# DeltaNet decays from gate sums in DRAM, loaded as broadcast rows

## What is computed

```python
def chunk_gated_delta(q, k, v, g, beta, s0):
    gc = jnp.cumsum(g, axis=-1)
    decay = jnp.exp(jnp.where(incl, gc[..., :, None] - gc[..., None, :], -jnp.inf))
    kb = k * beta[..., None]
    a_mat = (jnp.where(strict, jnp.einsum('bhnid,bhnjd->bhnij', kb, k) * decay, 0.0)
             + jnp.eye(DN_CHUNK, dtype=jnp.float32))
    ...
    qk = jnp.einsum('bhnid,bhnjd->bhnij', q, k) * decay

    def step(s, inp):
        v_new = u_i - jnp.einsum('bhcd,bhde->bhce', w_i, s)
        o_i = (jnp.einsum('bhcd,bhde->bhce', q_i * jnp.exp(g_i)[..., None], s)
               + jnp.einsum('bhij,bhje->bhie', qk_i, v_new))
```

## Time and profile before

| | us |
|---|---|
| median of 3 runs | 2942.37 |
| the runs | 2937.52 to 2944.89 |
| the profiled execution: its time | 2940.39 |
| the profiled execution: span of its instructions | 2938.8 |
| TensorE busy in it | 2628.8 |
| VectorE busy | 1885.0 |
| ScalarE busy | 1367.0 |
| GpSimd busy | 569.2 |

### The profile page before, as it was taken

One profiled execution on the slowest core, in us unless ns is written; L12 is line 12 of the kernel. 1 busy time (PEld: TensorE's weight loads), 2 busy tenths in 40 slices (PEclk: granted clock), 3 DMA queues, 4 the chain that ended last, 5 costly groups with the idle time before them and its releaser, 6 DMA issues. The chain is left out here.

```text
span 2938.8 us, 51977 instructions
## 1 busy us (share of the span) xinstructions
PE 2628.8 (89%) x17133; PEld 2420.6 (82%) x17133; DVE 1885.0 (64%) x3056; ACT 1367.0 (47%) x2263; POOL 569.2 (19%) x716
## 2 busy tenths in 40 slices
PE   2458999999999699999999999898999999998697
PEld 2458999999989598888888888898888888887597
DVE  3878888888853547665766566434576657665433
ACT  1024334434333535655565556323656555655522
POOL 2302222222211101221122112102112211221110
PEclk9999999999999799999999999999999999999899
DMA  8565666666653142222222222333222222221042
GB/s 237 188 222 201 233 230 229 228 229 232 227 177 128 57 147 69 74 69 68 68 75 71 69 70 68 123 124 133 65 75 68 71 71 68 75 71 50 20 156 93
DMA packets 115499, 362.09 MB, mean 123 GB/s; under 512 B 29056, under 2 KB 31232, under 8 KB 114560
## 3 DMA queue, kind: packets, MB, share of 16 engines
q1 hardware_dynamic: 69408, 252.74, 25.3%
q0 software_dynamic: 21200, 87.04, 8.8%
q10 hardware_dynamic: 24848, 21.76, 2.7%
HBM read 345.76 MB, written 15.73 MB: 123 GB/s over the span
## 5 line engine op out<-in xcount | busy, mean ns | idle before, releaser
L450 PE MATMUL bank<-h_hi,w_hi 128*128 128x384 f32 x2576 | 981.6, 381 | 48.0 <-DVE h_lo L1114 33.6
L452 PE MATMUL bank<-h_hi,w_lo 128*128 128x384 f32 x2576 | 872.3, 339 | 0.0
L451 PE MATMUL bank<-h_lo,w_hi 128*128 128x384 f32 x2576 | 871.2, 338 | 0.0
L418 DVE TENSOR_TENSOR w_lo<-raw,w_hi 128x1024 fp32r<-128x1024 f32 x418 | 555.2, 1330 | 443.4 <-ACT w_hi L410 406.9
L410 ACT ACTIVATE w_hi<-raw 128x1024 fp32r<-128x1024 f32 x418 | 442.0, 1060 | 455.8 <-PE bank L452 423.4
L450 PEld LDWEIGHTS bank<-h_hi,w_hi 128*128 128x128 f32 x2576 | 491.8, 191 | 71.3 <-issue 45.8
L451 PEld LDWEIGHTS bank<-h_lo,w_hi 128*128 128x128 f32 x2576 | 493.5, 192 | 13.5 <-issue 7.2
L452 PEld LDWEIGHTS bank<-h_hi,w_lo 128*128 128x128 f32 x2576 | 489.2, 190 | 0.0
L1079 DVE SCALAR_TENSOR_TENSOR ada_terms<-raw_ada,cond_rows 128x1024 f32<-128x1024 f32 x256 | 312.5, 1221 | 10.1 <-DMA raw_ada<-in_late 5.6
L450 PE MATMUL bank<-y_hi,w_hi 128*128 128x384 f32 x768 | 262.8, 342 | 29.2 <-DVE y_lo L1184 22.0
L451 PE MATMUL bank<-y_lo,w_hi 128*128 128x384 f32 x768 | 262.0, 341 | 0.0
(11 more groups left out here) (218 smaller groups left out, 3862.3 us busy)
## 6 DMA issues: line engine op xcount, KB each, us to landing
raw<-in_stream SPq DMA_DIRECT2D x482, 512.0 KB, 3.3
raw_ada<-in_late POOLq DMA_DIRECT2D x128, 512.0 KB, 3.6
x_kept<-y POOLq DMA_DIRECT2D x2, 3072.0 KB, 9.8
y<-x_kept POOLq DMA_DIRECT2D x2, 3072.0 KB, 10.3
bias<-in_rpb ACTq DMA_DIRECT2D x16, 256.0 KB, 6.5
S<-in_state ACTq DMA_DIRECT2D x16, 256.0 KB, 2.6
out_state_out<-s_out ACTq DMA_DIRECT2D x16, 256.0 KB, 2.1
y<-in_x ACTq DMA_DIRECT2D x1, 3072.0 KB, 20.0
```

The costliest lines, as they stand in the source:

```text
L418: nc.vector.tensor_tensor(w_lo[:, mk % SPLIT_SLOTS, :], raw[:, raw_n % RAW_SLOTS, :], w_hi[:, mk % SPLIT_SLOTS, :].bitcast(F32), ALU.subtr ...
L450: nc.tensor.matmul(bank[:, 0:T], w_hi[:, slot, w], hi[:, kt, :], start=kt == 0, stop=False)
L451: nc.tensor.matmul(bank[:, 0:T], w_hi[:, slot, w], lo[:, kt, :], start=False, stop=False)
L452: last = nc.tensor.matmul(bank[:, 0:T], w_lo[:, slot, w], hi[:, kt, :], start=False, stop=kt == KT - 1)
```

## The change

The gate sums are no longer formed once per head by products with triangles of ones. The phase `ba` forms them once for all heads: the table `gc` (tokens on the partitions) is a copy of the first `sums` product, and six products of the gates with the masks `le` and `ge` (`rows0`, `rows1`) give the same sums with the tokens along the row. ScalarE copies these and writes them to DRAM (`gc_rows`, 16 heads of 1536 numbers) with four DMAs. At the start of each head ScalarE, behind the load of the state, issues a load of the head's 6 KB to all 128 partitions (768 KB), into `decays`, one buffer that now holds the three `decay[c]`. Then:

- `broad` stands first in the list: ScalarE waits for that load and takes exp of chunks 1 and 2 straight from SBUF to `q_dec[c]`.
- `decay`: GpSimd subtracts the column of sums `gc_now` and cuts at 0, in place (four instructions per chunk), and ScalarE takes exp in place.
- The products of `decay` and `broad`, the masks of GpSimd and `g_now` are gone; `gc_now` is copied by VectorE at the start of the head. The ring's list is four places shorter (five gone, one place unused).
- `unit` has weight 3 and stands behind all three decays; with the other weights this leaves `norms`, `gram` and all that follows at the same part as before.

The diff, cut to its core:

```diff
-_chain = [(5, ("norms",)), (2.5, ("decay", 0)), (2, ("decay", 1)), (1.5, ("broad", 1)), (0, ("unit",)), (2, ("decay", 2)),
-          (1.5, ("broad", 2)), (1, ("gram", 0)), (2, ("gram", 1)), (2, ("gram", 2)), (1, ("values", 0)),
+_chain = [(0, ("broad", 1)), (0, ("broad", 2)), (5, ("norms",)), (2.5, ("decay", 0)), (2, ("decay", 1)), (2, ("decay", 2)),
+          (3, ("unit",)), (1, ("gram", 0)), (2, ("gram", 1)), (2, ("gram", 2)), (1, ("values", 0)),
           (1, ("values", 1))]
 for _stage in range(len(INVERT) - 1):
     _chain += [(3 if _stage < 2 and c < 2 - _stage else 2 if _stage < 2 else 1, ("invert", _stage, c)) for c in range(CHUNKS)]
...
+PRODUCTS += [("unused", "act")] * (-len(PRODUCTS) % RING)
...
-        g_now = sb("g_now", [P, CHUNKS, 2, 2])
+        gc_now = sb("gc_now", [P, CHUNKS, 2, 2])
+        gc = sb("gc", [P, CHUNKS, 2, DN_V_HEADS])
...
-        decay = [region.take(f"decay{c}", [P, 4, P]) for c in range(CHUNKS)]
+        decays = region.take("decays", [P, CHUNKS, 4, P])
+        decay = [decays[:, c, :, :] for c in range(CHUNKS)]
-        g_mask = [inv["c", c] for c in range(CHUNKS)]
+        gcT = overlay.take("gcT", [P, T])
-                                 "pool_waits", "v_out", "cache_k_in", "cache_v_in", "x0_in", "state_in", "state_out", "y_out")}
+                                 "pool_waits", "gc_out", "gc_in", "v_out", "cache_k_in", "cache_v_in", "x0_in", "state_in", "state_out", "y_out")}
...
+        def gc_loaded(eng, phase, turn):
+            eng.wait_ge(s["gc_in"], 16 * (turn + {"dn0": 1, "dn1": GROUP + 1, "dnE": 2 * GROUP}[phase]))
...
+            while PRODUCTS[n][0] == "unused":
+                n -= RING
...
+                for d, mask in enumerate(("le", "ge")):
+                    for c in range(CHUNKS):
+                        mm = nc.tensor.matmul(banks[6 + d][:, c * P:(c + 1) * P], bg[:, c, :], K[mask],
+                                              start=True, stop=True)
+                    done("pe", f"rows{d}", mm)
+
             def dn(pe, phase, turn):
                 for item in DN_PLANS[phase]:
                     what, arg = item[0], item[1] if len(item) > 1 else None
                     if what == "part":
                         multiply(pe, phase, turn, arg, item[2], h_hi, h_lo)
-                    elif what == "decay":
-                        wait_steps(pe, turn, ("pool", f"g_mask{arg}", True), ring_free(f"decay{arg}"))
-                        for d, mask in enumerate(("gt", "lt")):
-                            mm = nc.tensor.matmul(ring(f"decay{arg}")[:, 2 * d * P:(2 * d + 2) * P], K[mask],
-                                                  g_mask[arg][:, 2 * d:2 * d + 2, :].rearrange("p v i -> p (v i)"),
-                                                  start=True, stop=True)
-                        done("pe", f"decay{arg}", mm)
-                    elif what == "broad":
-                        wait_steps(pe, turn, ring_free(f"broad{arg}"))
-                        mm = nc.tensor.matmul(ring(f"broad{arg}")[:], K["ones"],
-                                              g_mask[arg][:].rearrange("p v i -> p (v i)"), start=True, stop=True)
-                        done("pe", f"broad{arg}", mm)
                     elif what == "norms":
                         for n in range(2):
                             wait_steps(pe, turn, ("pool", f"square{n}", True), ring_free(f"ss{n}"))
...
                     wait_steps(act, turn, ("pe", f"sums{n}"))
+                    if n == 0:
+                        done("act", "gc", nc.scalar.activation(gc[:].rearrange("p c d h -> p (c d h)"),
+                                                               banks[3][:, 0:CHUNKS * 2 * DN_V_HEADS], ACT.Copy))
                     done("act", f"table{n}", nc.scalar.activation(dst[:].rearrange("p c d h -> p (c d h)"),
                                                                   banks[3 + n][:, 0:CHUNKS * 2 * DN_V_HEADS], ACT.Exp))
+                for d in range(2):
+                    rows = slice(64 + 32 * d, 96 + 32 * d)
+                    wait_steps(act, turn, ("pe", f"rows{d}"))
+                    done("act", f"rows{d}", nc.scalar.activation(gcT[rows, :], banks[6 + d][rows, 0:T], ACT.Copy))
+                for d in range(2):
+                    wait_steps(act, turn, ("act", f"rows{d}"))
+                    for v in range(2):
+                        dst = bass.AP(dram["gc"].tensor, (2 * d + v) * P, [[CHUNKS * 4 * P, DN_K_HEADS], [4 * P, CHUNKS], [1, P]])
+                        src = gcT[64 + 32 * d + v:96 + 32 * d:2, :].rearrange("h (c i) -> h c i", c=CHUNKS)
+                        act.dma_start(dst, src).then_inc(s["gc_out"], 16)
             def dn(act, phase, turn):
                 head, _, _, row = heads(phase, turn)
...
+                    act.wait_ge(s["gc_out"], 16 * 4)
+                    act.dma_start(decays[:].rearrange("p c u i -> p (c u i)"),
+                                  dram["gc"][bass.ds(head, 1), :].broadcast_to([P, CHUNKS * 4 * P]))\
+                        .then_inc(s["gc_in"], 16)
                 def copy(name, dst, src, *others):
                     wait_steps(act, turn, ("pe", name), *others)
...
-                        wait_steps(act, turn, ("pe", f"decay{arg}"), ("pe", "outB", 1))
-                        done("act", f"decay{arg}", nc.scalar.activation(decay[arg][:].rearrange("p u i -> p (u i)"),
-                                                                        ring(f"decay{arg}")[:], ACT.Exp))
+                        wait_steps(act, turn, ("pool", f"below{arg}"))
+                        done("act", f"decay{arg}", nc.scalar.activation(decay[arg], decay[arg], ACT.Exp))
-                        wait_steps(act, turn, ("pe", f"broad{arg}"))
-                        done("act", f"broad{arg}", nc.scalar.activation(q_dec[arg][:].rearrange("p u i -> p (u i)"),
-                                                                        ring(f"broad{arg}")[:], ACT.Exp))
+                        gc_loaded(act, phase, turn)
+                        wait_steps(act, turn, ("pe", "outB", 1))
+                        done("act", f"broad{arg}", nc.scalar.activation(q_dec[arg][:], decay[arg], ACT.Exp))
...
+                    wait_steps(dve, turn, ("pool", "below2", True))
+                    done("dve", "gc_now", nc.vector.tensor_copy(gc_now[:], gc[:, :, :, bass.ds(2 * head, 2)]))
-                    elif what == "squares" and next_head is not None:
-                        wait_steps(dve, turn, ("pool", "g_mask2", True))
-                        done("dve", "g_now", nc.vector.tensor_copy(
-                            g_now[:], bg[:, :, 64:P].rearrange("p c (d h) -> p c d h", d=2)[:, :, :,
-                                                                                           bass.ds(2 * next_head, 2)]))
...
-                        wait_steps(dve, turn, ("dve", f"gram{c}"), ("act", f"decay{c}"), ("pe", f"broad{max(c, 1)}"),
-                                   ("pe", "applyB", True))
+                        wait_steps(dve, turn, ("dve", f"gram{c}"), ("act", f"decay{c}"), ("pe", "applyB", True))
...
-                    mask_steps(pool, turn)
...
-            def mask_steps(pool, turn, *which):
-                for c in range(CHUNKS):
-                    wait_steps(pool, turn, ("dve", "g_now"), *which)
-                    lone()
-                    for u in range(4):
-                        d, v = u // 2, u % 2
-                        i = nc.gpsimd.tensor_scalar(g_mask[c][:, u, :], K["le" if d == 0 else "ge"],
-                                                    g_now[:, c, d, v:v + 1], 1.0, ALU.mult, ALU.mult)
-                    done("pool", f"g_mask{c}", i)
...
-                        mask_steps(pool, turn, ("pe", "applyB"))
+                    elif what == "decay":
+                        gc_loaded(pool, phase, turn)
+                        wait_steps(pool, turn, ("dve", "gc_now"), *([("act", f"broad{arg}")] if arg else []))
+                        lone()
+                        for u in range(4):
+                            i = nc.gpsimd.tensor_scalar(decay[arg][:, u, :], decay[arg][:, u, :],
+                                                        gc_now[:, arg, u // 2, u % 2:u % 2 + 1], 0.0, ALU.subtract, ALU.min)
+                        done("pool", f"below{arg}", i)
...
+        dram["gc"] = nc.dram_tensor("gc_rows", (DN_K_HEADS, CHUNKS * 4 * P), F32).ap()

```

More of the change, by code:

```diff
@@ L208, in dn_products @@
         what, arg = item[0], item[1] if len(item) > 1 else None
-        if what == "decay":
-            made.append((f"decay{arg}", "act"))
-        elif what == "broad":
-            made.append((f"broad{arg}", "act"))
-        elif what == "norms":
+        if what == "norms":
             made += [("ss0", "act"), ("ss1", "act")]
@@ L1298, in dn @@
                         wait_steps(dve, turn, ("dve", f"c{c}"))
-                        both = decay[c][:].rearrange("p (d v) i -> p d v i", d=2)
```

(1 more changed line is left out.)

## The result

The changed kernel takes 3007.83 us (median of 4 runs, 3006.21 to 3009.76), the kernel before 2942.63 on the same chip (4 runs, 2937.52 to 2944.89): 1.022 times as long, 95% interval 1.021 to 1.024. The forecast was 2996, the range 2960 to 3030. The profiled execution took 3006.21 with a span of 3004.3, where that of before had 2938.8: 65.5 us more, against a sum of 54.3.

A forecast was written before the change was run, and what follows sets the result against it. TensorE's queue and a ScalarE-VectorE chain were taken to end together at gram. Steady heads 53.3, first heads -4.6, last head 2.8 and ba 2.8 gave 54.3 us on 2940.39: 2994.7, plus 2.0 to the median, said as 2996; range 2960 to 3030.

The forecast's parts named there:

- Products taken away: TensorE's queue ahead of gram: five steps at 0.86 us give 4.3 us a head, worthless unless the chain shortens.
- The load and the wait: Head start on ScalarE: decays land 4.5 us after S's issue; with exponentials, the weight half starts 3.5 us later.
- The table load: ScalarE at head start: one more Exp table load per head, about 1.28 us, hides under the wait for data.
- The clock: TensorE behind gram: 7.7 us of idling lowers its granted clock, costing 0.6 us a head, bounds 0 and 1.6.
- GpSimd: Twelve subtractions replace twelve masks in each head, take some 4 us, are over by 1291 and add nothing.
- First heads: First heads of dn0 and dn1: masks' wait gone, -2.9 and 0.6 for the clock, twice: -4.6 us.
- Last head: Last head, without weight halves: gram at 2715.0 instead of 2712.21, +2.8 us, bounds 0 and 5.6.
- ba: Stage ba: six more small products at 0.44 us each and a copy, +2.8 us, bounds 0 and 4.
- Products in full: Rival: TensorE's queue alone sets gram, 16 heads gain 4.3 us each, time near 2870; chance 0.04.
- Shift given back: Rival: TensorE's later waits in a head shrink by as much as gram comes late, time near 2943; chance 0.04.
- Transfer hidden: Rival: the load lands before the table load is over, shift 2.4 us, time near 2965; chance 0.08.
- Transfer slow: Rival: the 128 readings go as slowly as the first broadcast, landing at 7.3 us, time near 3050; chance 0.10.

The follow-up runs named there:

- narrow: Kernel before, with the products of its five decay and broad steps cut to 8 columns, waits, masks and exponentials kept: 2936.54 us, 0.9984 times before.
- unit_first: Kernel before, with unit (queries and keys scaled) moved from behind broad 1 to right behind norms: 2941.32 us, 1.0001 times before.
- tuned: Changed kernel with decays loaded at out_norm, unit right behind norms, exponentials spread behind it, subtractions on VectorE out of place: 2900.84 us, 0.9858 times before.
- late_exps: Changed kernel with the exponentials of broad 1 and 2 right behind norms instead of ahead of it: 2965.61 us, 1.008 times before.
- early_load: Changed kernel with the next head's load of decays issued at out_norm, once outB has read the buffer: 2978.96 us, 1.0129 times before.
- tuned_load_at_head: As tuned, but the load of decays is issued behind that of S at the head's start: 2902.85 us, 0.9879 times before.
- warm: Changed kernel with 42 extra TensorE products, overwritten later, ahead of its wait for the scaled keys in dn0 and dn1: 3000.9 us, 1.02 times before.
- tuned_pool: As tuned, but the twelve subtractions stay on GpSimd, also out of place: 2923.1 us, 0.9935 times before.

## Why the prediction was right

By its own steps:

- **What bounds the kernel.** Two paths that tie at `gram`. Shown by narrow and unit_first (neither alone moves a steady head) and by tuned (both move it by 2 us a head). Each had been seen to be as long to 0.2 us in the earlier trace rows; narrow found 0.16.
- **Products taken away.** 4.3 us for five steps. TensorE stands at 1394.67 (1402.61 - 7.94), 7.60 us after the issue of `S`; the step said 1289.5, 7.5 after. Right, and worth nothing without the chain, as the step said.
- **The load and the wait.** 4.5 us said, 4.78 measured in the head shown, 4.45 to 5.34 in the thirteen steady heads and 4.76 in the mean. The load's own issue comes 0.51 behind that of `S`, and it takes 4.2 from there in the median. This term was some 0.3 too small: the half starts 3.81 later in the head shown, not 3.5. The figures of the Trainium skill (DMA: Bandwidth & Descriptors, Anatomy of one DMA), given there for loads that GpSimd issues, had made the landing an estimated 4.2, further off. The Trainium skill (the same page, Rules for kernel authors) also asks to issue a load early and to wait late. Here late_exps bears out the late wait, and early_load the early issue for as long as the wait stands first. With the wait placed late, the early issue gained nothing in a steady head (tuned_load_at_head).
- **The table load.** The 2.66 us a switch of the Trainium skill (ScalarE: Activation LUTs, What ACT_TABLE_LOAD costs) would also have put the end of the wait at 4.8 us, but by another way. The rows decide against it: the load takes 1.28, and ScalarE is then idle for 1.36 until the data come. In early_load, where the data are there, the exponential starts 1.30 us after the table load did (1286.41, 1287.71).
- **The clock.** 0.6 said, 0.8 measured behind `gram`, of which warm gives 0.6 back; 0.72 of it is `gram` itself, where the step had looked for it. Steady heads in all: 59.4 instead of 53.3.
- **GpSimd.** Wrong in size. "Some 4 us, over by 1291" took the 0.37 us that a mask takes in the trace of before; the subtractions take 0.71 each, two of a head's twelve some 1.5 to 1.6 beside a `w_lo`: 9.97 us in all, over 15.0 us after the issue of `S`. That they add nothing held, with 2.15 us to spare on ScalarE. The step also feared a `w_lo` of 2.31 us beside them; both `w_lo` that they met took 1.23. tuned_pool shows the price when the cover is gone: 1.5 us a head.
- **First heads.** Head 0 gained 2.3 as said. Head 8 lost: +2.6 instead of -2.3. The step took the landing of a steady head there and left out the 3 MB write of `x` that GpSimd issues just before, and that the shorter barrier brings nearer. The barrier's own wait did shrink as forecast: from the last product of `outA` to the first of the head 8.43 us became 4.28 (2009.22 to 2017.65, 2040.29 to 2044.57). The crowded transfer is the one mechanism that was missed, 5 us.
- **Last head.** +4.2 to `gram` where 2.8 was said: landing 5.86 us after the issue of `S`, not 4.5 (ScalarE's exponential starts at 2770.94, `S` was issued at 2765.08); from there to `gram` 6.88, as the step had it. Only these two loads were in flight then, and why this one landed later than the others is open.
- **ba.** 2.8 said; TensorE's next stream product comes 2.9 later, and 2.4 are left at the end of `dnP`. The six new products, 2.91 us in twelve records:

```profile
1018.38 7.89 PE L661 MATMUL bank<-ada_terms,consts 128*128 128x32 f32 x36 [0.65 <-DVE ada_terms L1233]
1026.08 2.91 PE L667 MATMUL bank<-consts,ada_terms 128*128 128x128 f32 x12
```

- **Rivals.** Products in full: refuted by narrow, and by the result itself. Shift given back: `gram` to the next `S` grew by 0.8 and did not shrink. Transfer hidden: early_load is that case. It took 2979, and the 2965 of the rival does not follow from the prediction's own terms: 1.1 us less in each of 16 heads makes 54.3 into 36.7, which is 2979. That the total agrees so well is partly luck: the steady heads cost 42.5 us and not 39, and head 8 came out 3 us better. Transfer slow: the landing of 7.3 us was reached only in head 8 (11.1).

The sum missed 11 us: 6.1 in the steady heads, 4.9 in head 8, 2.2 in the last, less 0.4 in `ba` and 1.5 ahead of it.

## What to carry to other kernels

Where two paths end together, taking work from one gives nothing; read for each step of a change which of the two it shortens, and cut both in the same edit (here 40 and then 51 us, instead of 4 and none). In a queue that runs in order the price of a wait is that of the most urgent work behind it: here the wait for a load, with a table load and two exponentials behind it, cost 42 us more at the head of the list than behind `norms`, and once the wait stood late, the place of the issue made no difference clear of noise. And look at every place where a transfer is issued for what else is in flight, above all behind a barrier, instead of taking the median landing.

## What the runs showed of the hardware

- GpSimd's `tensor_scalar` on 128x128 float32 took 0.37 us as a product with a constant mask and 0.71 as subtraction and minimum, in place or not (medians). Beside a `w_lo` of VectorE the subtraction took 1.5 to 1.6, and the `w_lo` kept its 1.23. VectorE does it in 0.28, twelve in 2.44. Whether the operations or the source make the difference was not separated.
- A row of 6 KB in DRAM, read 128 times (768 KB), landed 3.9 to 4.8 us after its issue in the steady heads of the changed kernel, 4.2 in the median; 256 KB of `S` took 2.7 and 512 KB of weights 3.3. Behind a 3 MB write issued 3.45 us earlier on another queue it took 10.6.
- After a wait of 2.2 us the granted clock fell in twelve of thirteen steady heads, but cost 0.6 us behind `gram` only in every second one (narrow); after 5.2 and 7.9 us it cost this in every head. After 1.2 us (tuned) the granted clock stayed at 1.00.
